# Sorting the experts before the gates, loading and starting the first block earlier, and another order of rank capacities

## What is computed

```python
s = jax.nn.sigmoid(jnp.dot(h, w_router).astype(jnp.float32))
sb = s + b_router.astype(jnp.float32)
...                                   # 4 of 8 groups, then the 8 best experts in them
_, eidx = lax.top_k(jnp.where(emask, sb, -jnp.inf), TOP_K)
wts = jnp.take_along_axis(s, eidx, axis=1)
wts = wts / jnp.sum(wts, axis=-1, keepdims=True) * ROUTED_SCALE
...
def step(acc, blk):
    e, tok, wt = blk
    xb = h[tok]
    hb = jax.nn.silu(xb @ we_g[e]) * (xb @ we_u[e])
    return acc.at[tok].add(wt[:, None] * (hb @ we_d[e]).astype(jnp.float32)), None
...
shared = (jax.nn.silu(h @ ws_g) * (h @ ws_u)) @ ws_d
```

## Time and profile before

| | before |
|---|---|
| time, median of 3 runs | 1111.59 us (1110.45 to 1112.56) |
| time of the profiled execution | 1111.61 us |
| its span | 1109.8 us |
| TensorE busy | 1068.0 us (96%) |
| VectorE busy | 698.6 us (63%) |
| ScalarE busy | 218.0 us (20%) |
| GpSimd busy | 135.4 us (12%) |
| moved by DMA | 337.14 MB, 304 GB/s over the span |
| granted TensorE clock, mean | 0.994 |

### The profile page before, as it was taken

The page is one execution under the profiler, slowest core; times in us unless marked ns, Lnnn a source line. Parts: engine busy times, 40 slices in busy tenths (PEclk is TensorE's granted clock), DMA queues, the critical chain, the costliest instruction groups (busy, mean ns, idle before and its releaser), DMA issues.

```text
span 1109.8 us, 16863 instructions
## 1 busy us (share of the span) xinstructions
PE 1068.0 (96%) x6139; PEld 542.4 (49%) x6139; DVE 698.6 (63%) x1857; ACT 218.0 (20%) x478; POOL 135.4 (12%) x163
## 2 busy tenths in 40 slices
PE   6999999999999999999999999989999999899886
PEld 3456678777877644664343433333343333233232
DVE  3218441556545644862369888869888889688157
ACT  4131332322233213301111111101111111111111
POOL 0110000000020020111111121211111111111100
PEclk9999999999999999999999999989999999999999
DMA  9858721020262277869999999999999999999698
GB/s 368 337 203 305 232 80 45 32 86 4 112 197 80 76 243 248 313 220 421 404 425 424 424 425 422 425 423 410 414 426 422 425 424 423 422 420 387 243 419 341
DMA packets 51655, 337.14 MB, mean 304 GB/s; under 512 B 9637, under 2 KB 14089, under 8 KB 30831
## 3 DMA queue, kind: packets, MB, share of 16 engines
q1 hardware_dynamic: 33710, 287.32, 63.9%
q0 software_dynamic: 17856, 48.68, 11.6%
HBM read 311.30 MB, written 37.24 MB: 314 GB/s over the span
## 4 chain that ended last, share of the span: by engine, by line
PE 88%; DMA 7%; DVE 2%; issue 1%; ACT 1%; SPq 0%; DVEq 0%; POOLq 0%; ACTq 0%
PE bank L1565 29%; PE bank L1588 15%; PE bank L1260 10%; PE bank L1279 5%; DMA mem<-expert_out_rows 3%; PE bank L1378 3%; DMA mem<-in_w_exp_down 3%; PE bank L1379 3%; PE bank L1496 3%; PE bank L1173 3%; PE bank L1257 3%; PE bank L1148 1%; PE bank L1576 1%; PE bank L1131 1%; PE bank L1343 1%
## 5 line engine op out<-in xcount | busy, mean ns | idle before, releaser
L1565 PE MATMUL bank<-mem 128*32 128x512 f32 (+2 forms) x1504 | 330.3, 606 | 11.0 <-issue 10.4
L1565 PEld LDWEIGHTS bank<-mem 128*32 128x32 f32 (+2 forms) x1504 | 106.1, 129 | 191.8 <-issue 191.8
L2261 DVE STREAM_TRANSPOSE mem<-mem 32x256 f32<-32x256 f32 x400 | 174.2, 436 | 5.2
L1588 PE MATMUL bank<-mem 128*32 128x512 f32 (+2 forms) x752 | 164.4, 596 | 1.1 <-ACT mem L1069 1.1
L1260 PE MATMUL bank<-hT,mem 128*128 128x288 f32 x512 | 133.3, 409 | 1.0 <-ACT mem L939 1.0
L1565 PE MATMUL bank<-x_sb,mem 128*32 128x512 f32 (+2 forms) x400 | 111.2, 603 | 0.0
L1260 PEld LDWEIGHTS bank<-hT,mem 128*128 128x128 f32 x512 | 93.8, 190 | 25.8 <-issue 2.4
L2261 DVE STREAM_TRANSPOSE mem<-x_sb 32x256 f32<-32x256 f32 x208 | 90.6, 436 | 2.7
L1588 PEld LDWEIGHTS bank<-mem 128*32 128x32 f32 (+2 forms) x752 | 52.1, 127 | 72.1 <-issue 71.4
L2277 DVE COPY hT<-bank 128x512 f32<-128x512 f32 x48 | 33.2, 691 | 60.0 <-PE bank L1588 59.9
L1069 ACT ACTIVATE mem<-bank 128x256 f32<-128x256 f32 x48 | 18.4, 384 | 263.4 <-PE bank L1576 263.2
(11 more groups left out here) (404 smaller groups left out, 1258.1 us busy)
## 6 DMA issues: line engine op xcount, KB each, us to landing
mem<-k_w_exp SPq DMA_DIRECT2D x52, 2048.0 KB, 22.1
mem<-in_w_exp_down SPq DMA_DIRECT2D x52, 1024.0 KB, 23.8
x_sb<-k_w_exp SPq DMA_DIRECT2D x12, 2048.0 KB, 24.8
mem<-k_w_ada SPq DMA_DIRECT2D x8, 2048.0 KB, 9.3
mem<-k_w_in SPq DMA_DIRECT2D x7, 2048.0 KB, 8.9
hT<-in_w_exp_down SPq DMA_DIRECT2D x12, 1024.0 KB, 25.9
mem<-expert_out_rows SPq DMA_DIRECT2D x6, 2048.0 KB, 17.0
mem<-k_w_head SPq DMA_DIRECT2D x4, 2048.0 KB, 18.8
```

The lines of the kernel that those rows point to most:

```text
L1565: i = mm(bank[sl, :], xT[:, j % 2, c * BLK + sl.start:c * BLK + sl.stop], wview(r)[0][:, c, :], start=c == 0, stop=c == KC - 1)
L1588: i = mm(ps[4 + hf][sl, :], hhT[:, k * BLK + sl.start:k * BLK + sl.stop], wview(r)[1][:, k, hf * 512:(hf + 1) * 512], start=k == 0, stop=k ...
L2261: i = dve.transpose(cols[dl, :, sl], rows[sl, :, dl])
```

## The change

**Routing order.** On VectorE the scans come straight after the mask, then the sort, then the positions (`places`), then the token indices of block 0 alone (`first_tokens`, `token_out`, with the sorted ids between them), then shared_mul(0) and (1), and only then the gate weights and their parts (`gates`). idx_out(0) still writes the weights and scatter indices of block 0, but later. The copy of the positions' last row to `ovf` moves into `sort_keys`.

**TensorE.** After the positions: 6 shared steps, the sort product (now in bank 0), 3 steps, a token product of 2 columns (`find_tokens`), 12 steps, x_T(0), find_idx(0), find_idx(1), up(0), 5 steps, find_idx(2), then the blocks from x_T(1) on. The last 5 shared steps thus come after up(0).

**Memory and loads.** The shared weights and the router's move by 2048 elements, so that in slot 3 (LATESLOT) the down weights lie first, outside the shared weights, and the gate and up weights where these lie. SP loads rank 4's gate and up and rank 3's down weights at `tab_ready`, and after the last shared step rank 3's gate and up and rank 4's down weights; before it was both gate and up loads first, then both down loads.

**GpSimd.** The spread of the last gain rows (`bcG`) moves from behind the first gather to ahead of the gathers. The first gather waits for `tok_ready`. Its steps are counted on the semaphore `over` in place of `pool_step`.

**Capacities.** CAPS holds the same numbers in another order; the first three are the same.

The diff, cut to its core:

```diff
-CAPS = [4, 4, 4,
-        2, 2, 1, 3, 3, 1, 4, 5, 3, 3, 2, 3, 4, 4, 3, 2, 3, 3, 2, 3, 3, 2, 3, 4, 4, 3, 5, 3, 2, 3, 3, 2, 3, 4, 4, 6, 2, 2,
-        2, 4, 1, 3, 6, 2, 5, 3, 4, 2, 2, 3, 2, 3, 8, 2, 2, 1, 3, 2, 2, 2, 2]
+CAPS = [4, 4, 4, 3, 1, 2, 1, 2, 3, 6, 2, 2, 2, 4, 3, 2, 3, 4, 2, 6, 3, 3, 2, 3, 2, 3, 4, 3, 3, 2, 5, 3, 1, 3, 5, 3, 3, 2, 3, 4,
+        4, 3, 3, 3, 3, 4, 2, 8, 2, 4, 4, 2, 3, 2, 5, 2, 2, 1, 3, 4, 2, 2, 2, 2]
...
+LATESLOT = 3
...
-        gu_s, e_ = carve(mem, v_at, [2, KC, FE])
+        gu_s, e_ = carve(mem, w2_at + FJ * D, [2, KC, FE])
...
+            if slot(r) == LATESLOT:
+                gu = mem[:, at_ + FJ * D:at_ + WSZ].rearrange("p (c n) -> p c n", c=KC)
+                return gu, mem[:, at_:at_ + FJ * D].rearrange("p (j d) -> p j d", j=FJ)
...
-            load_gate_up(NPRE, id3)
             load_gate_up(XSLOT, id4)
+            load_dn(LATESLOT, id3)
             sp.wait_ge(S["gu_mm"], NSH)
-            load_dn(NPRE, id3)
+            load_gate_up(LATESLOT, id3)
             load_dn(XSLOT, id4)
...
             pool.wait_ge(S["h2T_t"], NT)
+            pool.wait_ge(S["ld_bc"], 3 * SPREAD + 16)
+            spread(pool, bcG, 5, S["ld_bc"])
...
             def ahead(n, q, g):
-                pool.wait_ge(S["idx_ready"], n + 1)
+                if isinstance(n, int) and n == 0:
+                    pool.wait_ge(S["tok_ready"], 1)
+                else:
+                    pool.wait_ge(S["idx_ready"], n + 1)
...
-            shared_up(12)
+            shared_up(6)
+            def find_tokens():
+
+                pe.wait_ge(S["P_ready"], 1)
+                pe.wait_ge(S["pos_done"], 1)
+                pe.wait_ge(S["gu_silu"], 2)
+                for tt in range(NT):
+                    i = mm(ps[6][:, 0:2], Pm[:, 0, tt, :], Re[:, 0, tt, 0, 0:2], start=tt == 0, stop=tt == NT - 1)
+                i.then_inc(S["pos_mm"], 1)
...
+            pe.wait_ge(S["srt_ready"], 1)
+            pe.wait_ge(S["gu_silu"], 1)
+            mm(ps[0][:, 0:2 * NE], ones[0:NE, :], sperm[0:NE].rearrange("p a e -> p (a e)"),
+               start=True, stop=True).then_inc(S["srt_mm"], 1)
+            shared_up(3)
+            find_tokens()
+            shared_up(12)
+            x_T(0)
             find_idx(0, 0, pieces(0))
-            shared_up(4)
             find_idx(1, 1, pieces(1))
-            shared_up(KC // 2)
-            pe.wait_ge(S["sh_ready"], 2)
-            pe.wait_ge(S["srt_ready"], 1)
-            mm(ps[7][:, 0:2 * NE], ones[0:NE, :], sperm[0:NE].rearrange("p a e -> p (a e)"),
-               start=True, stop=True).then_inc(S["srt_mm"], 1)
-            shared_up(KC // 2)
-            x_T(0)
-            shared_up(2)
+            new_gu(0)
+            up(0, 0, pieces(0))
+            shared_up(5)
             find_idx(2, 2, pieces(2))
...
+            def first_tokens():
+
+                cp(Re[:, 0, :, 0, 0:2], Rk[:, :, 0:4:3, 0])
+                stt(Pm[:, 0], pos[:, :, 0:1].to_broadcast([P, NT, P]), 0.0, iota.unsqueeze(1).to_broadcast([P, NT, P]),
+                    ALU.add, ALU.is_equal).then_inc(S["P_ready"], 1)
+
+            def token_out():
+
+                dve.wait_ge(S["pos_mm"], 2)
+                o = ps[6]
+                ts(idxg[:, 0:1], o[:, 0:1], o[:, 1:2], float(OOB), ALU.add, ALU.add).then_inc(S["tok_ready"], 1)
...
-            place(0)
-            place(1)
-            idx_out(0, 0)
+            assert SEGS[0] == [(0, P // QS, 0, 0)]
+            sort_keys()
+            places()
+            first_tokens()
+            sorted_ids()
+            token_out()
             for i in range(2):
                 shared_mul(i)
-            sort_keys()
+            gates()
+            shared_mul(2)
+            cp(Re[:, 0, :, 0, :], Rk[:, :, :, 0])
+            place(1)
+            xT_evac(0, 0)
+            idx_out(0, 0)
             idx_out(1, 1)
-            shared_mul(2)
-            sorted_ids()
             place(2)
-            xT_evac(0, 0)
             shared_mul(NSH - 1)
             idx_out(2, 2)
```

More of the change, by code:

```diff
@@ L802, in ahead @@
                     pool.wait_ge(S["xT_ready"], n - XG + 1)
-                pool.sem_inc(S["pool_step"], 1)
+                pool.sem_inc(S["over"], 1)
                 gather(q, g)
@@ L818, in _ @@
                 ahead(n, n, n)
-                if n == 0:
-                    pool.wait_ge(S["ld_bc"], 3 * SPREAD + 16)
-                    spread(pool, bcG, 5, S["ld_bc"])
             for b in range(NBK):
@@ L1527, in _ @@
             positions()
-            shared_up(12)
-            def find_idx(n, j, parts):
-                pe.wait_ge(S["P_ready"], n + 1)
-                if not (isinstance(n, int) and n == 0):
+            shared_up(6)
[6 more added lines that the diff above has]
+                i.then_inc(S["pos_mm"], 1)
+            def find_idx(n, j, parts):
+                if isinstance(n, int) and n == 0:
+                    pe.wait_ge(S["P_ready"], 2)
+                    pe.wait_ge(S["tok_ready"], 1)
+                else:
+                    pe.wait_ge(S["P_ready"], n + 1)
                     pe.wait_ge(S["idx_ready"], n)
-                else:
-                    pe.wait_ge(S["pos_done"], 1)
-                    pe.wait_ge(S["gu_silu"], 2)
                 for tt in range(NT):
@@ L1624, in _ @@
             for b in range(NBK):
-                new_gu(b)
                 split = KC if b + 1 < TURNED else KC - 2
-                up(b, b, pieces(b), range(split))
+                if b >= 1:
+                    new_gu(b)
+                    up(b, b, pieces(b), range(split))
                 if b == 0:
@@ L2136, in _, with places @@
                 dve.tensor_tensor_scan(cumv[:, t, :], ones[:, 0:NE], maskm[:, t, :], 0.0, ALU.mult, ALU.add)
-            step(cp(R[:, 1], sbias))
-            step(tt_(sbias, sbias, R[:, 1], ALU.subtract))
-            step(cp(R[:, 4], sbias))
-            tt_(R[:, 6], sbias, R[:, 4], ALU.subtract)
-            tt_(R[:, 5], R[:, 7], cumv, ALU.add)
-            dve.wait_ge(S["pos_mm"], 1)
+            def places():
+                dve.wait_ge(S["pos_mm"], 1)
+                step(stt(pos, PV[:, 0:NT, :], FAR, maskm[:, 0:NT, :], ALU.add, ALU.mult))
+                ts(pos, pos, -FAR, None, ALU.add).then_inc(S["pos_done"], 1)
+                dve.wait_ge(S["pos_done"], 1)
@@ new lines, in gates @@
+            def gates():
+                step(tt_(sbias, smat, maskm[:, 0:NT, :], ALU.mult))
+                dve.tensor_reduce(stat[:, 12, 0:NCH], sbias[:, 0:NCH, :], AX.X, ALU.add)
+                step(dve.tensor_reduce(stat[0:NS, 12, NCH:NT], sbias[0:NS, NCH, :], AX.X, ALU.add))
+                step(dve.reciprocal(stat[:, 13, :], stat[:, 12, :]))
+                step(stt(sbias, sbias, ROUTED, stat[:, 13, :].unsqueeze(2).to_broadcast([P, NT, NE]), ALU.mult, ALU.mult))
+                step(cp(R[:, 1], sbias))
+                step(tt_(sbias, sbias, R[:, 1], ALU.subtract))
+                step(cp(R[:, 4], sbias))
+                tt_(R[:, 6], sbias, R[:, 4], ALU.subtract)
+                step(tt_(R[:, 5], R[:, 7], cumv, ALU.add))
@@ L2242, in idx_out @@
                 o = ps[6]
-                ts(idxg[:, q:q + 1], o[:, 0:1], o[:, 3:4], float(OOB), ALU.add, ALU.add)
+                if not (isinstance(n, int) and n == 0):
+                    ts(idxg[:, q:q + 1], o[:, 0:1], o[:, 3:4], float(OOB), ALU.add, ALU.add)
                 ts(wtab[:, q:q + 1], o[:, 1:2], o[:, 4:5], o[:, 6:7], ALU.add, ALU.add)
```

19 lines of the change are left out of this document (6 added, 13 removed).

## The result

| | before | after |
|---|---|---|
| time, median | 1112.07 us (1110.45 to 1114.91, 4 runs) | 1128.41 us (1127.84 to 1130.56, 4 runs) |
| profiled execution: time, span | 1111.61, 1109.8 us | 1130.56, 1128.7 us |
| rank 8's gate and up load issued at | 527.94 | 541.51 |

After is slower: the ratio is 1.0143, with a 95% interval of 1.013 to 1.0156. The forecast was 1117, with a range to 1122.5. The direction was right and the size three times too small. The profiled execution of the changed kernel was the slowest of its four, 2.2 us over the median. Times of rows are again from the start of the span; two executions of one kernel can differ by about 1 us in them ahead of the stage.

A forecast was written before the change was run, and what follows sets the result against it. The weight stream was taken to set the end, last held by up(3)'s end at 527.94. Head +8.1 and order -2.5 sum to +5.6 us on 1111.59, giving 1117, range 1108.5 to 1122.5.

The forecast's parts named there:

- Whatever moves up(3) moves the end one for one: Rank 8's load waits for up(3)'s end, 527.94; any shift of up(3) shifts the kernel's end equally.
- The early 3 MB: Weights for ranks 4 and 3 arrive sooner, but nobody needs them before block 3: worth nothing.
- rival (3): Weight stream keeps its early 3 MB and the end moves by up to -6 us, to 1105.5; faster, chance 0.17.
- The head, +8.1 us: Delay at the third block's transposes, x_T(2), and the same at up(3); low end +1.0, high end +13.3.
- The first gather: Issued at 478.95 just ahead of 3 MB of weights, lands in 7.6 us, bounds 4.4 and 10.8; TensorE waits 5.9.
- The clock: Slower TensorE clock after the 5.9 us idle ahead of up(0) costs 2.4 us; bounds 0 and 2.9.
- From up(0)'s end to up(1)'s start: up(1) starts 12.2 us after up(0) did, before 9.54; TensorE idles 2.6 us there.
- The third gather: Issued behind three new loads, takes 10 us; rows 20.85 us after up(0) starts, wanted at 19.35.
- The order, -2.5 us: New capacity order issues rank 63's gate and up load earlier, ahead of two down loads; bounds 0 and -4.7 us.
- From there on it never does: After rank 8's load at 527.94 the weight pipe never runs dry again.
- Case (4): Both gathers and the clock at their high ends, +13.3, no order gain: 1125 us; chance 0.13.
- a test that I set: If rank 8's load lands in more than 10 us, the argument that early bytes don't count is wrong.

The follow-up runs named there:

- the sort alone: The changed kernel with the old order of capacities (old CAPS): 1126.95 us, ratio 1.0125.
- both edits: Changed kernel, old CAPS, loads of ranks 4 and 3 held until the first gather landed, last five shared steps ahead of the first transposes: 1123.62 us.
- the index products first: As the run with both edits, plus index products of blocks 0 and 1 ahead of the first transposes, block 2's ahead of up(0): 1117.51 us.
- the filled wait: Changed kernel with 22 or 11 further products that nothing reads in the first gather's wait: 1128.16 us and 1124.57 us.
- moving the eight late: Kernel before with the new order of capacities, the eight-quarter rank 47 exchanged with rank 55: 1117.38 us, ratio 1.004.
- steps first: The changed kernel with the last five shared steps moved back ahead of the first transposes: 1124.99 us, ratio 1.0111.
- gather first: The changed kernel, its sync queue waiting for the first gather's rows before loading weights of ranks 4 and 3: 1121.14 us, ratio 1.0075.
- 11 products in the wait: The changed kernel with 11 further 128x288 products, results unread, in the first gather's wait: 1124.57 us, ratio 1.0106.
- 22 products in the wait: The changed kernel with 22 further 128x288 products, results unread, in the first gather's wait: 1128.16 us.

## Why the prediction was wrong, point by point

**Whatever moves up(3) moves the end one for one: right.** With the old order it held to 0.24 us in three runs (the sort alone, both edits, the index products first), and the medians of the filled wait agree. The early 3 MB were worth nothing, and rival (3) didn't come about: with the early loads, nothing was issued between 480.14 and 505.44.

**The head, +8.1 us: right mechanism, terms mis-sized.** Measured 13.56, which is 5.4 more.

- The first gather: I took the middle, 7.6 us, because "this gather meets the stream's beginning, not a backlog". It took 9.66. Its start was forecast at 478.95 and was 480.12; half a microsecond of that is TensorE's shared steps, which held back the token product. Together the transposes started at 489.83, forecast at 486.55: 3.28 us. The rule of the Trainium skill that the forecast weighed against this term ("DMA: Bandwidth & Descriptors", Queues, rings and completion order: an engine alternates between queue rows packet by packet) would have put it near 4.4. The trace does not agree with that: 9.66 beside the loads, 4.5 in the run without them. Where all rows of a kind that met loads stood at 10 and 11.5, the middle towards the one that had not was the wrong choice.
- The clock: "I take 2.4", measured 0.93 + 2.60 + 1.54 = 5.07, 2.67 us more. The rows gave the loss on the one product right behind a wait. Here the transposes and the first product lost 3.5 behind 5.45 us of idle time, and the second product lost again behind 1.91 + 0.40. I priced one wait and there were two. The lower bound, "0 (for a wait of under 3 us)", had no row behind it: the wait of 2.94 us in the earlier trace rows cost 1.75.
- From up(0)'s end to up(1)'s start: 5.1 - 2.43 = 2.67 us more than before were forecast, 3.63 came, 0.96 more. TensorE's idle time there was forecast at 2.6 and was 2.31. The rest is the step "six shared steps at 6.07/24 = 0.25 us each": the row's 24 matmuls are 12 steps, two for each, so a step takes 0.51 us, and the five behind up(0) took 2.59 us, where 1.25 was in the sum.
- The third gather: 1.5 us of wait forecast, none came (517.61 has no bracket). TensorE was by then so late that the rows, 8.4 us after their issue at 507.80, were there.

The misses are 3.28 + 2.67 + 0.96 - 1.5 = 5.4. The same wrong step length is why the waits forecast ahead of the sort product and the token product, 1.4 and 0.6 us, did not come. That the wait for the first rows came out near its forecast, 5.45 us against 5.9, is luck: TensorE was ready for them at 484.38 and not at 480.65, and they came 3.2 us late.

**The order, -2.5 us: wrong sign.** The step that failed is "From there on it never does", said of the pipe running dry. With the old order it does at 1000 to 1010 (336 GB/s). That lies in the 37th slice of the earlier trace rows, 387, which the forecast left out of its eighteen full slices and took for the stream's end; but the last gate and up load is issued later, at 1015.95. The gain was then worked out at the last load alone, as if the stream came to it full. It comes to it 3.6 us poorer than before. Measured: +4.4 us for the order alone. In the profiled execution of the changed kernel 13.6 + 4.4 = 18.0 us stand at the last down product. The size is less sure than the sign: by the medians the changed kernel is 16.3 us above the kernel before and 14.4 (1126.95 - 1112.51) with the old order, so the order costs 1.9 there. From rank 8's load to the last down product the six profiled executions with the new order as it is and whole down products took 2.2 to 5.0 us more than the kernel before, the three with the old order and a changed head 0 to 0.2 less.

**What the range left out.** Case (4), both gathers and the clock at their high ends with no gain from the order, gave 1125 and is the nearest; only a cost of the order was in no case.

**Also wrong: a test that I set.** Rank 8's load landed in 10.1 us, and I had written that over 10 would refute that early bytes don't count. The one-for-one shift refutes the test instead: the rate at 541 to 543 was 340 GB/s, well below the full rate, so the pipe had room, though less than before.

Shown are: the one-for-one shift, the gather's 5 us as the loads' doing, the clock as idle time's doing, the sign of the order, that moving the eight late moves its dry stretch and not the price, and that TensorE's pace carries a good part of the order's cost. Only argued is why a stretch goes dry: all free slots are full, and the next comes free when a long rank ends. Open are which places in the list carry the cost, how much of it VectorE's pace holds, and why the order costs less in the changed kernel's medians. No version that computes the whole layer beat the kernel before.

## What to carry to other kernels

A small gather that the critical engine waits for must have landed before the bulk loads start, or leave early enough to be hidden behind other work; leaving 1.4 us ahead of them did not make it quick here. And a bulk load issued earlier is worth nothing if the next one waits for the same buffer anyway. Price the clock behind every wait of the engine, not just the longest. Before a static order is changed, look at the transfer rate in stretches no longer than one block: the order may already be losing there, and a gain at its last element counts only if the stream comes to it full.

## What the runs showed of the hardware that was not expected

**The clock behind equal waits.** Transposes and first up product, and then the second, by the idle time ahead of each:

| kernel | idle ahead | transposes, up product | idle ahead of the second | second product |
|---|---|---|---|---|
| after | 5.45 | 1.97, 9.71 | 1.91 + 0.40 | 8.65 |
| after, old order | 5.16 | 1.97, 9.28 | 2.07 + 0.26 | 10.05 |
| steps first | 3.79 | 1.26, 9.59 | 1.54 + 0.40 | 7.10 |
| gather first | 0.29 | 1.09, 7.11 | 1.75 + 0.40 | 8.80 |
| 11 products in the wait | 0.32 | 1.09, 7.11 | 1.91 + 0.40 | 8.57 |
| 22 products in the wait | 0 | 1.04, 7.11 | 1.91 + 0.40 | 7.11 |

In these runs the waits of 3.79 us and longer cost 2.7 to 4.0 us in what followed (the most in the run with both edits: 5.59 us, then 1.94 and 10.17). Waits of 1.9 to 2.3 us in two parts cost between nothing and 2.9: with the same 1.91 + 0.40 it was 0, 1.46 and 1.54. The Trainium skill, "TensorE: Matmul & The Clock Gate", Part 1, says that the slow clock is the default which activity lifts, and that one kernel can show other numbers of slow products from run to run; these rows agree with the second as far as kernels that differ only ahead of the wait can tell.

**Gathers beside the stream.** A gather of 128 rows took 4.0 to 4.5 us with the queues empty, and 9.4 to 9.9 together with the first 3 MB of loads, which alone need 7.4 us at the full rate (10.4 in the run with the steps first, where the next 3 MB followed at 486.63). Issued 1.36 us ahead of the first of four loads, 6 MB in all, it took 10.8 us. Behind 6 MB issued from 484.6 to 486.9 (485.1 to 487.4 in the run with both edits) the second gather took 8.8 us, and about 11.2 (489.75 to 500.96). So a gather can end later than a load that it met: in the changed kernel its rows were there at 489.78, the first 2 MB at 487.8 and the 1 MB behind them at 490.5.
